# Channel sums folded on VectorE ahead of one matmul each, and the delta rule's first chunk without its zero state

## What is computed

```python
def layer_norm(x, w, b):
    mu = jnp.mean(x, axis=-1, keepdims=True)
    xc = x - mu
    y = xc * lax.rsqrt(jnp.mean(xc * xc, axis=-1, keepdims=True) + EPS)
    return y * w + b

    y_b = rms_norm(rglru_mixer(...), grp_norm_w[l, 0])
    y_c = rms_norm(sgu_mixer(...), grp_norm_w[l, 1])       # layer_norm is inside
    y_d = rms_norm(short_conv_mixer(...), grp_norm_w[l, 2])
```

```python
def step(state, inp):
    q_i, a_i, u_i, w_i, k_i, gl_i = inp
    v_new = u_i - w_i @ state
    o_i = q_i @ state + a_i @ v_new
    state = state * gl_i + k_i.T @ v_new
    return state, o_i
s0 = jnp.zeros((Bn, H, Dk, Dv))
_, o = lax.scan(step, s0, xs)
```

## Time and profile before

| what | value |
|---|---|
| median of 3 runs | 3407.18 us |
| lowest and highest | 3406.81 and 3407.94 us |
| span of the profiled execution | 3407.3 us, all the time of it that is shown |
| mean granted clock of PE | 0.997 of full speed |
| w_in with the mixer | about the first 346 us of the span |

### The profile page before, as it was taken

How to read it: one execution, slowest core, us unless ns; L and a number is a source line. 1 busy time by engine, 2 the same in 40 slices (tenths; PEclk the granted TensorE clock), 3 DMA queues, 4 the chain that set the end, 5 groups by cost and what they waited for, 6 DMA issues and landing times.

```text
span 3407.3 us, 59138 instructions
## 1 busy us (share of the span) xinstructions
PE 3380.9 (99%) x19590; PEld 2953.4 (87%) x19590; DVE 2250.2 (66%) x2934; ACT 1746.8 (51%) x2591; POOL 541.1 (16%) x508
## 2 busy tenths in 40 slices
PE   9999999999999999999999999999999999999999
PEld 7898888888888888888888888888888888888888
DVE  7868687777754475555555599856687656556544
ACT  5445565555544455445444455544566544444433
POOL 1204111111100011111100056611100111111000
PEclk9999999999999999999999999999999999999999
DMA  6524545555566645555566655554556555555665
GB/s 210 161 94 147 189 152 185 190 190 186 188 187 190 189 157 187 185 191 189 186 184 191 215 173 177 181 167 157 171 192 196 188 188 186 187 192 186 185 192 171
DMA packets 175601, 616.16 MB, mean 181 GB/s; under 512 B 20864, under 2 KB 21408, under 8 KB 175136
## 3 DMA queue, kind: packets, MB, share of 16 engines
q1 hardware_dynamic: 175088, 609.84, 55.7%
q10 hardware_dynamic: 432, 5.24, 0.4%
HBM read 610.81 MB, written 4.19 MB: 180 GB/s over the span
## 4 chain that ended last, share of the span: by engine, by line
PE 95%; DVE 2%; issue 1%; ACT 1%; DMA 0%; POOL 0%; DVEq 0%; SPq 0%; POOLq 0%; ACTq 0%
PE acc L393 60%; PE acc L396 30%; DVE weights_low L279 1%; PE acc L408 1%; PE ps_scale L603 1%; PE ps_narrow L2297 0%; PE ps_wide L2273 0%; ACT weights_high L272 0%; PE acc L411 0%; DVE halves_memory L494 0%; PE ps_wide L1380 0%; PE ps_wide L1426 0%; PE ps_wide L1390 0%; PE ps_wide L1384 0%; DMA weights_raw<-in_w_diff_branch 0%
## 5 line engine op out<-in xcount | busy, mean ns | idle before, releaser
L393 PE MATMUL acc<-moving_halves,weights_high 128*128 128x512 f32 x6400 | 2039.6, 399 | 1.8 <-DVE x_T L2566 1.8
L279 DVE TENSOR_TENSOR weights_low<-weights_raw,weights_high 128x1024 fp32r<-128x1024 f32 (+2 forms) x1184 | 1450.0, 1237 | 738.0 <-ACT weights_high L272 736.7
L272 ACT ACTIVATE weights_high<-weights_raw 128x1024 fp32r<-128x1024 f32 (+2 forms) x1184 | 1220.6, 1032 | 797.5 <-PE acc L396 771.6
L396 PEld LDWEIGHTS acc<-moving_halves,weights_low 128*128 128x128 f32 x6400 | 1204.1, 188 | 284.2
L396 PE MATMUL acc<-moving_halves,weights_low 128*128 128x256 f32 x6400 | 1259.3, 278 | 0.0
L393 PEld LDWEIGHTS acc<-moving_halves,weights_high 128*128 128x128 f32 x6400 | 980.3, 189 | 13.3 <-issue 9.8
L393 PE MATMUL acc<-gated_halves,weights_high 128*128 128x512 f32 x2024 | 635.6, 395 | 0.0
L488 ACT ACTIVATE cross_products<-acc 128x256 f32<-128x256 f32 x509 | 194.6, 382 | 693.8 <-PE acc L396 693.7
L396 PEld LDWEIGHTS acc<-gated_halves,weights_low 128*128 128x128 f32 x2024 | 380.2, 188 | 89.9
L511 POOL TENSOR_TENSOR stage_scratch<-unscaled,token_scale 128x256 f32<-128x256 f32 x264 | 217.9, 826 | 1302.6 <-DVE unscaled L494 778.2
L396 PE MATMUL acc<-gated_halves,weights_low 128*128 128x256 f32 x2024 | 397.6, 278 | 0.0
(11 more groups left out here) (361 smaller groups left out, 1972.3 us busy)
## 6 DMA issues: line engine op xcount, KB each, us to landing
weights_raw<-in_w_in SPq DMA_DIRECT2D x271, 512.0 KB, 4.0
weights_raw<-in_ffn_up SPq DMA_DIRECT2D x176, 512.0 KB, 4.3
weights_raw<-in_ffn_w_gate SPq DMA_DIRECT2D x176, 512.0 KB, 4.1
weights_raw<-in_ffn_w_up SPq DMA_DIRECT2D x176, 512.0 KB, 4.6
weights_raw<-in_ffn_w_down SPq DMA_DIRECT2D x160, 512.0 KB, 3.9
weights_raw<-in_ffn_down SPq DMA_DIRECT2D x80, 512.0 KB, 4.2
weights_raw<-in_w_out SPq DMA_DIRECT2D x64, 512.0 KB, 3.8
weights_raw<-in_ffn_w_down SPq DMA_DIRECT2D x32, 256.0 KB, 2.7
```

The lines of the kernel that those rows point to most:

```text
L272: core.nc.scalar.activation(core.high[:, slot, k0:nk, :].rearrange("p a b -> p (a b)"), core.raw[:, slot, k0 * P:nk * P], ACT.Copy).then_i ...
L279: core.nc.vector.tensor_tensor(core.low[:, slot, k0:nk, :].rearrange("p a b -> p (a b)"), core.raw[:, slot, k0 * P:nk * P], core.high[:, s ...
L393: core.nc.tensor.matmul(acc[:, t % 2, :, :], core.high[:, u % SLOTS, k, :], parts[:, prod.first[t] + k0 + k, :, :], start=(k0 + k == 0), s ...
L396: core.last = core.nc.tensor.matmul(acc[:, t % 2, 0, :], core.low[:, u % SLOTS, k, :], parts[:, prod.first[t] + k0 + k, 0, :], start=False ...
```

## The change

`channel_sum` now takes only a number. DVE first adds the four tiles in one `tensor_reduce` into `self.channels` (128x256, in the stage's scratch memory), and PE does one matmul with the ones behind it. A new semaphore `added` carries the order. The four tiles lie 256 or 260 elements apart, and the reduce is along them, so it reads every element from another place than the one before. The sums of n=1, 3 and 4 move one or two slots later on PE (60 to 62, 72 to 73, 83 to 84), `stat` moves for n=1 (61 to 62), 3 (73 to 74) and 4 (84 to 85), the refinement for n=1 from slot 63 to 64, and ACT's root for n=1 goes behind `take_o(3)`.

For chunk 0 of the delta rule `state_part(0)` and the four products of q with the state are gone, `new_values(0)` and `next_state(0)` are plain copies, and the memset of the state is gone.

```diff
+        self.channels = core.scratch[:, 0:S]
...
-                nc.tensor.matmul(pb[:, h, 0:CHUNK], self.state[:, h, :], qT[:, 2 * h + half, rows], start=True, stop=False)
+                if n:
+                    nc.tensor.matmul(pb[:, h, 0:CHUNK], self.state[:, h, :], qT[:, 2 * h + half, rows], start=True, stop=False)
                 last = nc.tensor.matmul(pb[:, h, 0:CHUNK], v_new[:, h, :], self.attnT[:, 2 * h + half, rows],
-                                        start=False, stop=True)
+                                        start=(n == 0), stop=True)
...
-        def channel_sum(out, src):
-            for j in range(4):
-                last = nc.tensor.matmul(out, core.c("ones"), src[:, j, :], start=(j == 0), stop=(j == 3))
-            return last
+        def channel_sum(n):
+            pe.wait_ge(self.added, n + 1)
+            nc.tensor.matmul(self.p_stat[:, n % 2, :], core.c("ones"), self.channels, start=True,
+                             stop=True).then_inc(self.channel_sums, 1)
...
         pe.wait_ge(self.w_out, 1)
-        state_part(0)
...
         outputs(0)
-        pe.wait_ge(self.gelu_done, 2)
-        channel_sum(self.p_stat[:, 0, :], self.tiles(SGU_V)).then_inc(self.channel_sums, 1)
+        channel_sum(0)
...
         state_part(2)
-        pe.wait_ge(self.sq_done, 1)
-        channel_sum(self.p_stat[:, 1, :], self.spare4).then_inc(self.channel_sums, 1)
...
         state_part(3)
+        channel_sum(1)
...
-        yield from s.at(83)
+        channel_sum(3)
+        yield from s.at(84)
         pe.wait_ge(self.stat_ready, 3)
-        pe.wait_ge(self.sq_done, 4)
-        channel_sum(self.p_stat[:, 0, :], self.lru_i).then_inc(self.channel_sums, 1)
+        channel_sum(4)
...
+        def add_channels(src):
+            nc.vector.tensor_reduce(self.channels, src.rearrange("p j s -> p s j"), AX, ALU.add).then_inc(self.added, 1)
...
         yield from s.at(72)
+        dve.wait_ge(self.sq_done, 3)
+        add_channels(lru_r)
         group_norm(0, LRU_X)
-        yield from s.at(73)
+        yield from s.at(74)
         stat(3, self.p_stat[:, 1, :])
...
         yield from s.at(83)
+        dve.wait_ge(self.sq_done, 4)
+        add_channels(lru_i[:, :, :])
         for k in range(4, 8):
             self.part_low(dve, k)
-        yield from s.at(84)
+        yield from s.at(85)
         stat(4, self.p_stat[:, 0, :])
```

More of the change, by code:

```diff
@@ L1270, in __init__ @@
                  "o_out", "state_ready"))
-        (self.centred, self.channel_sums, self.gelu_done, self.lru_acted, self.lru_args, self.lru_gates,
+        (self.added, self.centred, self.channel_sums, self.gelu_done, self.lru_acted, self.lru_args, self.lru_gates,
          self.mixed, self.out_done, self.rx_done, self.sc_done, self.sc_own, self.sg_done, self.sq_done,
@@ L1274, in __init__ @@
             core.sem(f"mix_{s}") for s in
-                ("centred", "channel_sums", "gelu_done", "lru_acted", "lru_args", "lru_gates",
+                ("added", "centred", "channel_sums", "gelu_done", "lru_acted", "lru_args", "lru_gates",
                  "mixed", "out_done", "rx_done", "sc_done", "sc_own", "sg_done", "sq_done", "stat_ready",
@@ L1394, in state_part @@
             half, rows = delta(n)
-            pe.wait_ge(self.state_ready, n + 1)
+            pe.wait_ge(self.state_ready, n)
             for h in range(HEADS):
@@ L1565, in tensor @@
         pe.wait_ge(self.stat_ready, 1)
-        pe.wait_ge(self.sq_done, 2)
-        channel_sum(self.p_stat[:, 0, :], self.conv[:, 12:16, :]).then_inc(self.channel_sums, 1)
-        yield from s.at(72)
+        channel_sum(2)
+        yield from s.at(73)
         pe.wait_ge(self.stat_ready, 2)
-        pe.wait_ge(self.sq_done, 3)
-        channel_sum(self.p_stat[:, 1, :], self.lru_r).then_inc(self.channel_sums, 1)
-        yield from s.at(83)
+        channel_sum(3)
+        yield from s.at(84)
         pe.wait_ge(self.stat_ready, 3)
-        pe.wait_ge(self.sq_done, 4)
-        channel_sum(self.p_stat[:, 0, :], self.lru_i).then_inc(self.channel_sums, 1)
+        channel_sum(4)
     def scalar(self, act):
@@ L1685, in scalar @@
         nc.scalar.activation(self.lru_r, self.lru_r, ACT.Sqrt).then_inc(self.lru_acted, 1)
-        stat_root(1)
         yield from s.at(63)
         take_o(3)
+        stat_root(1)
         yield from s.at(64)
@@ L1800, in new_values @@
             u_by = self.u_sb.rearrange("p (h a) d -> p h a d", a=HALVES)
-            dve.wait_ge(self.ws_done, n + 1)
             if n == 0:
                 dve.wait_ge(self.pool_done, 3)
+                nc.vector.tensor_copy(self.v_new[r][rows, :, :], u_by[rows, :, half, :]).then_inc(self.vn_ready, 1)
+                return
+            dve.wait_ge(self.ws_done, n)
             nc.vector.tensor_tensor(self.v_new[r][rows, :, :], u_by[rows, :, half, :], pa[rows, 0:HEADS, :],
@@ L1809, in next_state @@
             dve.wait_ge(self.st_done, n + 1)
+            if n == 0:
+                nc.vector.tensor_copy(self.state[:, :, :], pa[:, HEADS:2 * HEADS, :]).then_inc(self.state_ready, 1)
+                dve.wait_ge(self.state_ready, 1)
+                return
             for h in range(HEADS):
@@ L1814, in next_state @@
             last.then_inc(self.state_ready, 1)
-            dve.wait_ge(self.state_ready, n + 2)
+            dve.wait_ge(self.state_ready, n + 1)
+        def add_channels(src):
+            nc.vector.tensor_reduce(self.channels, src.rearrange("p j s -> p s j"), AX, ALU.add).then_inc(self.added, 1)
         def stat(n, src):
@@ L1911, in vector @@
         nc.vector.tensor_tensor(self.b_diag, over_units(core.c("ident")), each_column(beta8), ALU.mult).then_inc(self.diag, 1)
-        nc.vector.memset(self.state[:, :, :], 0.0).then_inc(self.state_ready, 1)
         yield from s.at(36)
@@ L1966, in vector @@
         new_values(0)
+        dve.wait_ge(self.gelu_done, 2)
+        add_channels(self.tiles(SGU_V))
         yield from s.at(57)
@@ L1994, in vector @@
         dve.wait_ge(self.centred, 1)
-        stat(1, self.p_stat[:, 1, :])
+        dve.wait_ge(self.sq_done, 1)
+        add_channels(self.spare4)
         yield from s.at(62)
         new_values(3)
+        stat(1, self.p_stat[:, 1, :])
         yield from s.at(63)
@@ L2000, in vector @@
         own.add(nc.vector.tensor_tensor(lru_i[:, :, :], lru_i[:, :, :], lru_r, ALU.mult))
+        yield from s.at(64)
         stat_newton(1)
-        yield from s.at(64)
         for j in range(4):
@@ L2014, in vector @@
         nc.vector.tensor_tensor(a, t, self.tiles(LRU_G), ALU.mult).then_inc(self.out_done, 1)
+        yield from s.at(67)
+        dve.wait_ge(self.sq_done, 2)
+        add_channels(conv[:, 12:16, :])
         yield from s.at(69)
@@ L2030, in vector @@
         yield from s.at(72)
+        dve.wait_ge(self.sq_done, 3)
+        add_channels(lru_r)
         group_norm(0, LRU_X)
-        yield from s.at(73)
+        yield from s.at(74)
         stat(3, self.p_stat[:, 1, :])
-        yield from s.at(74)
         for k in range(4):
```

## The result

The changed kernel takes 3412.66 us (median of 21 runs, 3410.93 to 3413.95); beside it the kernel before takes 3407.18 us (21 runs, 3405.59 to 3409.1). The ratio is 1.0016, 95% interval 1.001 to 1.0022. Forecast were 3406.3 us and a range up to 3410.5, so the change costs 5.5 us where a gain of 0.9 was expected, and the time lies outside the range. It is still under the 0.2% named there.

The account below looks back on a forecast made before the run. PE, busy 99%, was taken as the bound. Of 8.2 us removed, plus 0.27 us of waiting, waits and delays left 0.95: 3407.3 - 0.95 is 3406.35 us by the span, 3406.3 by the median, range 3403 to 3410.5.

Parts of the forecast that it names:

- I take 1.22 us: DVE's new reduce of 1024 elements: 1.22 us each, from rows of contiguous reduces, with nothing extra for the large step.
- gain when chunk 69 begins: Slots 56 to 69: 5.9 us saved on PE less 1.1 us of new waits, net 4.8 us.
- wait in slot 73: PE stands still 2.7 us ahead of the sum of n=3, until DVE's reduce is ready.
- gain when chunk 74 begins: Behind slot 73's wait and sum, the gain falls from 4.8 to 4.1 us.
- wait in slot 84: PE stands still 3.9 us for DVE's last reduce, ahead of the sum of n=4.
- gain when chunk 85 begins: Behind slot 84, between 1.5 and 2.7 us of gain are left; 1.9 was taken.
- the tail: End of the mixer: the later stat(4) delays ACT's next rounding by 0.95 us, so 1.9 us of gain become 0.95.
- A fall after slot 73 is free, since PE waits in slot 84 anyway: A lower PE clock behind slot 73's wait costs no time; only one after slot 84 costs, up to 2.7 us.
- no further wait comes of that: Slots 73 on: DVE work queued behind the reduce causes no wait, as PE needs chunk 77 only at about 313.
- I take a third of the way: Group norm of 304.25, pushed 1.22 us back, runs less beside POOL: gain between 1.5 and 2.7 us, taken as 1.9.
- The clock: Rival, 15 in 100: the new waits lower PE's clock; a fall after slot 84 costs up to 2.7 us, giving 3409.0.
- The strided read: Rival, 13 in 100: the reduce costs double, 2.44 us, adding 4.4 us through slots 62, 68, 73 and 84, giving 3410.7.

Follow-up runs that it names:

- e5: Changed kernel with the reduce adding four neighbouring elements instead of the four tiles, so its output is not the reference's: 3407.53 us, ratio 1.0004.
- e1: Kernel before with only the delta rule's part of the change, all five channel sums still four matmuls: 3405.73 us, ratio 0.9997.
- e2: Changed kernel with the sums of n=3 and n=4 as before, four matmuls in slots 72 and 83: 3403.79 us, ratio 0.9991.
- e4: Changed kernel with 7 and 10 matmuls whose results nobody reads in PE's waits of slots 73 and 84: 3409.13 us, ratio 1.0007.
- e9: Kernel before, nothing folded, with only the sum and stat of n=4 moved a slot later: 3407.76 us, ratio 1.0001.
- e6: Changed kernel with the reduce replaced by two tensor_tensor additions, three for n=0: 3412.76 us, ratio 1.0018.
- e7: Changed kernel with DVE's last reduce one slot earlier, in slot 82 instead of 83: 3409.19 us, ratio 1.0007.
- e3: Kernel before with only the sums of n=3 and n=4 folded and placed as in the change: 3415.76 us, ratio 1.0026.
- e8: Kernel before with only the sum of n=3 folded: 3409.73 us, ratio 1.0009.

## Why the prediction was wrong

**"I take 1.22 us"** for a reduce: this step failed first. It read the strided copy of 16 elements as a sign that steps cost nothing. 1024 elements took 1.93 us, 0.7 ns an element more. On 16 elements that is 0.011 us, and a row of another instruction, a copy held against a line for reduces, can't exclude so little. The text had said that the row could hide a third of a nanosecond; in the reduce it is twice that. e5 and the changed kernel differ in nothing but the step, and its penalty is 1.6 times here, not 2. The Trainium skill (Advanced Engine Details and Errata, SBUF Cachelines) names a penalty for such reads without a size. By that rule the trace agrees; how small the step must be to go without it was not tried.

With the reduce at the predicted length, e5 tests the working that hung on it. Counted from slot 55's matmuls:

| term | predicted | e5 | after |
|---|---|---|---|
| gain when chunk 69 begins | 4.8 | 4.96 | 3.63 |
| wait in slot 73 | 2.7 | 2.73 | 3.43 |
| gain when chunk 74 begins | 4.1 | 4.34 | 2.0 |
| wait in slot 84 | 3.9 | 4.51 | 4.69 |
| gain when chunk 85 begins | 1.9 | 0.91 | -3.1 |

The net gain of slots 56 to 69 and the wait of slot 73 were right; within the former the wait of slot 62, put at 0.5 us, is about 0.1 in e5. The removed work was worth what was said: e1 gives 1.72 of S for the delta rule's 1.76 in matmuls, and e2, which holds e1's part, 3.68.

The size of the reduce is not all of the miss. The forecast's 0.95 us of gain would be an S of 216.4, and e5 has 218.83. Of these 2.4 us, 1.0 is lost by the start of chunk 85. From there to the end of S e5 takes 106.19 us against 103.80 before, 2.4 more, where the forecast had 0.95 for the tail: the rest is the clock behind slot 84.

**"A fall after slot 73 is free, since PE waits in slot 84 anyway"** and **"no further wait comes of that"** were wrong, and they are one error: both take a late PE to leave DVE alone. From the start of the group norm (before) or the reduce ahead of it to DVE's next landmark in slot 83, DVE took 338.04 - 304.25 = 33.79 us before and 337.88 - 300.31 = 37.57 after. DVE's timeline after:

```profile
300.31 1.91 DVE L1820 TENSOR_REDUCE stage_scratch<-arena 128x256 f32<-128x1024 f32 x1
302.13 2.08 DVE L1835 SCALAR_TENSOR_TENSOR arena<-arena,vectors,squares_total 128x256 f32<-128x256 f32 x4
...
308.54 1.23 DVE L279 TENSOR_TENSOR weights_low<-weights_raw,weights_high 128x1024 fp32r<-128x1024 f32 x1 [2.86 <-ACT weights_high L272]
...
312.94 0.96 DVE L1778 TENSOR_TENSOR squares<-squares_total 128x256 f32<-128x256 f32 x1
313.94 1.40 DVE L1780 SCALAR_TENSOR_TENSOR squares<-squares 128x256 f32<-128x256 f32 x1
315.38 0.58 DVE L1782 SCALAR_TENSOR_TENSOR squares_total<-squares,squares_total 128x256 f32<-128x256 f32 x1
```

Before, DVE's longest gap in that stretch was 0.45 us. Now it stands idle for 2.86 us, for the rounding of chunk 78. ACT's timeline after shows whom ACT waited for:

```profile
307.44 1.06 ACT L272 ACTIVATE weights_high<-weights_raw 128x1024 fp32r<-128x1024 f32 x1 [2.78 <-PE acc L396]
```

It waited for PE to leave chunk 74, which PE began late, after its wait, and did at half clock. With four buffers, what PE loses in slot 73 stops ACT and then DVE, which reaches the last reduce later. The forecast had PE's lateness vanish inside the wait of slot 84; DVE carried it on instead. In e5, with a shorter wait and no fall of the clock there, DVE's idle time is 0.72 us. How much of the 2.86 is the wait's and how much the clock's was not tried apart.

**"I take a third of the way"** for POOL's relief, 0.4 us, had a term missing. The group norm fell from 3.75 to 2.08 us, nearly all of the way. But `stat(3)`'s refinement, moved one low part later, takes 0.96 + 1.40 + 0.58 = 2.94 us, where the same three took 0.41 + 0.50 + 0.42 = 1.33 before. POOL had rows beside both, but other ones. The longest of the three before, what POOL ran beside it, and POOL's timeline beside the first two of the three after:

```profile
314.53 0.50 DVE L1784 SCALAR_TENSOR_TENSOR squares<-squares 128x256 f32<-128x256 f32 x1
```
```profile
313.49 2.78 POOL L2082 TENSOR_SCALAR lru_w<-arena,vectors 128x256 f32<-128x256 f32 x2
```
```profile
311.85 1.77 POOL L511 TENSOR_TENSOR arena<-unscaled,token_scale 128x256 f32<-128x256 f32 x1 [1.30 <-DVE unscaled L494]
313.58 1.48 POOL L2101 TENSOR_TENSOR arena<-arena,lru_w 128x512 f32<-128x512 f32 x1
```

Beside POOL's `tensor_scalar` they were hardly slowed, beside its `tensor_tensor` they were. Relief and burden, 1.67 and 1.61, cancel in the changed kernel; that they do is luck. In e5, where the group norm took 2.69 us and the refinement 2.94, they come to 0.55 us of loss. With DVE's 0.72 us of idle time, less 0.46 by which the next group norm was shorter (3.40 to 2.94), that is 0.8 us of loss where the forecast had 0.4 of gain: about what is missing at chunk 85. The forecast looked only at what was moved out of POOL's way, not at what was moved into it.

**The clock** was a rival with 15 in 100, priced as up to 2.7 us after slot 84 alone. It came true after both waits, and e4 gives 2.8 us of S for both (3.5 by the medians). **The strided read** was a rival with 13 in 100. The forecast took them as alternatives, together only in its 4 in 100 for a slower kernel. Both came true, and by e5's trace they are linked: with the shorter reduce the wait of slot 73 left the clock alone. e5 (3.7 us) and e4 (2.8) overlap there, so they may not be added, and no run has both. The tail's 0.95 us was near: 0.69 in e9.

## What to carry to other kernels

Where one engine is 99% busy, ask of work moved off it whether its result is needed at once: the three early sums, with waits of at most 0.83 us, gave 1.96 us, and the two with waits of 3.43 and 4.69 cost 8.83, though all five spare PE the same. In a ring of buffers a stall of the bound engine also stops the engines that feed it, so price a wait with what comes back through the buffers, and with the clock behind it. Ask what the other engines run where the moved work lands, too. A price read from a row of 16 elements doesn't carry to 1024; where a row of like size is missing, the larger bound belongs in the forecast itself.

## What the runs showed of the hardware

- DVE's reduce of 1024 float32 into 256 takes 1.205 us from neighbours and 1.88 to 1.95 us with steps of 256 or 260 elements, with POOL at work (1.91) or without a record (1.93).
- Two DVE adds with both inputs in SBUF (e6) took 0.68 and 0.42 us with POOL quiet, and 1.75 and 1.37 us beside two `tensor_tensor` of POOL. Three instructions of a refinement took 1.33 us beside POOL's `tensor_scalar` and 2.94 beside its `tensor_tensor`.
- PE's clock fell to 0.50 after waits of 3.43 and 4.69 us. It fell after 2.05 us too (e7, a mean of 0.59 in the stretch behind it), but not after 2.73 us (e5). After the same wait it is not low equally long: in two stretches of 4 us behind a wait of 3.4 us the means are 0.50 and 0.78 in e3, and 0.57 and 1.00 in e8. The length of the wait alone doesn't decide; what does stays open here.
- Unread matmuls in both waits kept the clock at 1.00 (e4) and gave back 2.8 us of S.
